# Attention scores of two heads issued together, alternating between the two partition halves

## What is computed

```python
# fox, and alike for the others: scores of the queries [start, end) with the keys [0, end)
s = jnp.einsum('bqhd,bkhd->bhqk', q[:, start:end], k[:, :end]).astype(jnp.float32) * scale
bias = c[:, :, start:end, None] - c[:, :, None, :end]      # fox only: c = cumsum(log_sigmoid(f))
p = jax.nn.softmax(jnp.where(mask, s + bias, -jnp.inf), axis=-1)
outs.append(jnp.einsum('bhqk,bkhd->bqhd', p.astype(v.dtype), v[:, :end]))
# index heads: rel = relu(iq . ik); score = sum over heads of rel * iw; top_k picks the keys of dsa
```

## Time and profile before

| | us |
|---|---|
| median of 3 runs | 2168.05 |
| lowest, highest | 2159.57, 2171.18 |
| the profiled execution | 2163.28 |
| its span | 2161.6 |
| PE busy in the span | 2056.4 (95%) |
| DVE busy | 1469.4 (68%) |
| ACT busy | 976.2 (45%) |

### The profile page before, as it was taken

How to read it: one execution, slowest core, us unless ns; L and a number is a source line. 1 busy time by engine, 2 the same in 40 slices (tenths; PEclk the granted TensorE clock), 3 DMA queues, 4 the chain that set the end, 5 groups by cost and what they waited for, 6 DMA issues and landing times.

```text
span 2161.6 us, 35906 instructions
## 1 busy us (share of the span) xinstructions
PE 2056.4 (95%) x13708; PEld 1878.8 (87%) x13708; DVE 1469.4 (68%) x2592; ACT 976.2 (45%) x1464; POOL 36.9 (2%) x72
## 2 busy tenths in 40 slices
PE   7999999999999999999989997998899979898998
PEld 6999998879998999998879996897789968787997
DVE  7776557677767776557678776765766668566665
ACT  5334444643344344544644344554444445544443
POOL 0000000000000000000000000000000000000000
PEclk9999999999999999999999998996999999878999
DMA  8774443157764774442247762530345544213553
GB/s 303 274 264 165 176 156 109 68 185 277 276 237 160 277 283 183 159 166 101 85 169 274 275 224 97 180 116 32 135 176 194 187 153 152 103 68 125 187 185 135
DMA packets 76906, 382.15 MB, mean 177 GB/s; under 512 B 8960, under 2 KB 9088, under 8 KB 55552
## 3 DMA queue, kind: packets, MB, share of 16 engines
q1 hardware_dynamic: 67392, 329.78, 41.6%
q0 software_dynamic: 9408, 50.90, 6.8%
HBM read 379.60 MB, written 1.05 MB: 176 GB/s over the span
## 4 chain that ended last, share of the span: by engine, by line
PE 87%; DVE 8%; ACT 3%; issue 2%; DMA 0%; SPq 0%; DVEq 0%; ACTq 0%
PE psum L534 26%; PE psum L535 26%; PE psum L536 26%; DVE weights_low_a L1280 2%; PE psum L718 1%; PE psum L713 1%; PE psum L780 1%; PE psum L805 1%; PE psum L807 1%; PE psum L806 1%; PE psum L833 1%; DVE h_low L1331 1%; ACT weights_high_a L955 1%; PE psum L627 1%; PE psum L625 1%
## 5 line engine op out<-in xcount | busy, mean ns | idle before, releaser
L534 PE MATMUL psum<-h_high,weights_high_a 128*128 128x256 f32 x2480 | 713.3, 288 | 15.8 <-DVE h_low L1327 7.7
L535 PE MATMUL psum<-h_low,weights_high_a 128*128 128x256 f32 x2480 | 705.2, 284 | 0.0
L536 PE MATMUL psum<-h_high,weights_low_a 128*128 128x256 f32 x2480 | 704.6, 284 | 0.0
L1280 DVE TENSOR_TENSOR weights_low_a<-raw_a,weights_high_a 128x2048 fp32r<-128x2048 f32 (+1 forms) x232 | 460.1, 1984 | 108.4 <-ACT weights_high_a L955 105.8
L534 PEld LDWEIGHTS psum<-h_high,weights_high_a 128*128 128x128 f32 x2480 | 478.3, 193 | 31.3 <-issue 12.1
L535 PEld LDWEIGHTS psum<-h_low,weights_high_a 128*128 128x128 f32 x2480 | 479.0, 193 | 7.0 <-issue 1.0
L536 PEld LDWEIGHTS psum<-h_high,weights_low_a 128*128 128x128 f32 x2480 | 478.5, 193 | 0.0
L955 ACT ACTIVATE weights_high_a<-raw_a 128x2048 fp32r<-128x2048 f32 (+1 forms) x232 | 387.1, 1669 | 160.5 <-PE psum L536 157.2
L1280 DVE TENSOR_TENSOR weights_low_b<-raw_b,weights_high_b 128x1024 fp32r<-128x1024 f32 x224 | 273.6, 1221 | 78.5 <-ACT weights_high_b L955 77.4
L955 ACT ACTIVATE weights_high_b<-raw_b 128x1024 fp32r<-128x1024 f32 x224 | 237.5, 1060 | 162.2 <-PE psum L536 162.2
L534 PE MATMUL psum<-weights_high_b,gated_high 128*128 128x512 f32 x608 | 241.1, 397 | 0.0
(11 more groups left out here) (276 smaller groups left out, 2897.0 us busy)
## 6 DMA issues: line engine op xcount, KB each, us to landing
ada_weights<-in_w_ada POOLq DMA_DIRECT2D x64, 768.0 KB, 5.1
raw_a<-in_w_ffn_a_a SPq DMA_DIRECT2D x44, 1024.0 KB, 7.2
raw_a<-in_w_ffn_b_a SPq DMA_DIRECT2D x44, 1024.0 KB, 7.3
raw_a<-in_w_ffn_a SPq DMA_DIRECT2D x64, 512.0 KB, 4.5
raw_b<-in_w_ffn_b SPq DMA_DIRECT2D x64, 512.0 KB, 3.5
raw_a<-in_w_proj_a SPq DMA_DIRECT2D x28, 1024.0 KB, 5.7
raw_a<-in_w_gate_a SPq DMA_DIRECT2D x26, 1024.0 KB, 4.7
raw_b<-in_w_ffn_a_b SPq DMA_DIRECT2D x44, 512.0 KB, 3.6
```

The costliest lines, as they stand in the source:

```text
L534: pe.matmul(out, l_hi, r_hi, start=start, stop=False, skip_group_check=True)
L535: pe.matmul(out, l_hi, r_lo, start=False, stop=False, skip_group_check=True)
L536: return pe.matmul(out, l_lo, r_hi, start=False, stop=stop, skip_group_check=True)
L1280: dve.tensor_tensor(wlo[kind][:, p, 0:width], raw[kind][:, p, 0:width], whi[kind][:, p, 0:width].bitcast(F32), ALU.subtract).then_inc(lo_r ...
```

## The change

Heads h and h+1 (h even) of one kind that stand next to each other in the list of items are a pair: their scores are issued together in the first one's tick, product by product in turns, each head into its own bank (ticks t and t+1 have different banks). `scores_ready` (or `prep_ready` for idx) is still raised once per head, by its last product; for fox the forget products of the first half also take turns, those of the second half are issued head by head. The waits of both ticks (`bank_free` for t and t+1) stand ahead of the pair, so it waits for item t-1 to be read besides item t-2. The second head's tick then has no scores on PE. In block 1 kv moves ahead of fox 0, so that fox 0 and fox 1 are neighbours at ticks 2 and 3. Single heads (sb 4, dsa 4) stay as they were. DVE's and ACT's code is the same but for the name of the bank constant and the place of fox 0 and kv in the list.

```diff
-    items = [("ckv", 0), ("fox", 0), ("kv", 0), ("fox", 1), ("turn", 0), ("turn", 1)]
+    items = [("ckv", 0), ("kv", 0), ("fox", 0), ("fox", 1), ("turn", 0), ("turn", 1)]
...
+def paired(items, tick):
+
+    kind, h = items[tick]
+    return kind in HEADS + ("idx",) and h % 2 == 0 and tick + 1 < len(items) and items[tick + 1] == (kind, h + 1)
...
-                while back >= 0 and items[back] is None:
-                    back -= 2
                 if back >= 0:
...
+            def scores(blk, items, ticks_):
+
+                with_forget = items[ticks_[0]][0] == "fox"
+                last = {}
+                for tick in ticks_:
+                    q, k_ = score_operands(items[tick])
+                    pe.matmul(ps[:, SCORE_BANKS[tick % 2], 0:P], q[:, 0:P], k_[:, 0:P], start=True,
+                              stop=not with_forget, skip_group_check=True)
+                if with_forget:
+                    for tick in ticks_:
+                        pe.matmul(ps[:, SCORE_BANKS[tick % 2], 0:P], fcast[:, items[tick][1], 0, :],
+                                  consts[:, C_U:C_U + P], start=False, stop=True, skip_group_check=True)
+                for tick in ticks_:
+                    q, k_ = score_operands(items[tick])
+                    last[tick] = pe.matmul(ps[:, SCORE_BANKS[tick % 2], P:3 * P], q[:, P:SEQ], k_[:, 0:SEQ], start=True,
+                                           stop=not with_forget, skip_group_check=True)
+                for tick in ticks_:
+                    if with_forget:
+                        bank, h = SCORE_BANKS[tick % 2], items[tick][1]
+                        pe.matmul(ps[:, bank, P:3 * P], fcast[:, h, 0, :], consts[:, C_U:C_U + SEQ],
+                                  start=False, stop=False, skip_group_check=True)
+                        last[tick] = pe.matmul(ps[:, bank, 2 * P:3 * P], fcast[:, h, 1, :], consts[:, C_U:C_U + P],
+                                               start=False, stop=True, skip_group_check=True)
+                    if items[tick][0] == "idx":
+                        last[tick].then_inc(now().prep_ready, 1)
+                    else:
+                        last[tick].then_inc(now().scores_ready, 1)
...
             def item_scores(blk, items, tick):
                 kind, h = items[tick]
-                bank = 2 + tick % 2
-                bank_free(items, tick)
+                if tick and paired(items, tick - 1):
+                    return
+                both = (tick, tick + 1) if paired(items, tick) else (tick,)
+                for t in both:
+                    bank_free(items, t)
...
+                if kind in HEADS or kind == "idx":
+                    scores(blk, items, both)
+                    return
+                bank = SCORE_BANKS[tick % 2]
```

More of the change, by code:

```diff
@@ L55 @@
 ROW_BANKS = 6
+SCORE_BANKS = (2, 3)
 P1_G, P1_GKV, P1_BF, P1_GIDX, P1_WKV, P1_END = 0, 24, 25, 31, 95, 223
@@ L709, in bank_free, with score_operands @@
                     pe.wait_ge(s, count_upto(items, back, lambda k: READ_BY[k] == kind))
[L711 to L725, removed]
+            def score_operands(item):
+                kind, h = item
+                q, k_ = {"fox": lambda: (qk1[:, 0, h // 2, :], qk1[:, 1, h // 2, :]),
+                         "sb": lambda: (qk1[:, 2, h // 2, :], qk1[:, 3, h // 2, :]),
+                         "idx": lambda: (tt1[:, h // 2, :], tt1[:, 2, :]),
+                         "dsa": lambda: (tt1[:, 4 + h // 2, :], tt1[:, 3, :]),
+                         "swa": lambda: (tt2[:, h // 2, :], tt2[:, 4 + h // 4, :]),
+                         "moba": lambda: (tt2[:, 6 + h // 2, :], tt2[:, 10 + h // 2, :])}[kind]()
+                pb = HD * (h % 2)
+                return q[pb:pb + HD, :], k_[pb:pb + HD, :]
@@ L734, in item_scores @@
                 if kind in ("kv", "idx", "dsa", "swa", "moba"):
-                    before = max(i for i in range(tick) if items[i] and items[i][0] in ("ckv", "kv", "turn"))
+                    before = max(i for i in range(tick) if items[i] and items[i][0] in PREP and items[i][0] != "idx")
                     pe.wait_ge(now().prep_copied, count_upto(items, before, lambda k: k in PREP))
+                if kind in HEADS or kind == "idx":
+                    scores(blk, items, both)
+                    return
+                bank = SCORE_BANKS[tick % 2]
                 m = None
[L739 to L756, removed]
                 if kind == "ckv":
```

## The result

The changed kernel takes 2142.03 us, median of 4 runs from 2140.90 to 2143.64; the kernel before took 2167.77 beside it. The ratio is 0.9893, 95% interval [0.9872, 0.9914]; the quotient of the two medians, 0.9881, lies inside it. The forecast was 2144, "faster". The profiled execution has a span of 2140.0 us, against 2161.6.

What follows compares the result with a forecast made beforehand. PE was taken as the bound, except in the second half of block 1's ticks. Two layers of 6.5 us (block 2) and 4.4 us (block 1) take 21.8 off 2165.7: 2144, own range 2134 to 2153, with rivals 2129 to 2157.

Steps and rivals of the forecast that it cites:

- Costs of a head and of a pair: Scores on PE: a plain head 1.04 us, fox head 2.31; pairing saves 1.03 per plain pair, 1.42 per fox pair.
- c = 0.22 and s = 0.19: On PE, us for 128 columns of an f32 product, and us lost per switch between 64-row and 128-row products.
- The two equations: PE cost of one head's scores: plain 3c + 2s = 1.04 us, fox 7c + 4s = 2.31 us.
- Block 2 with gate tiles, 4.1 per layer: Four swa pairs at ticks 2, 5, 7 and 9 save 1.03 us each, 4.1 per layer.
- Block 2 without them, 2.4 per layer: Ticks 16 to 25: pairs at 19 and 21 drop 1.58 us each, other engines take back 0.7; 2.4 left.
- Block 1, 4.9 up to tick 14, 4.4 at the end: Per layer, pairs up to tick 14 gain 4.9 us; later savings become PE waits, the tail takes 0.5, leaving 4.4.
- the ring of the earlier trace: Block 1's sb heads: DVE and ACT wait for each other (1.15, 1.88 us) without PE; later PE savings become waits.
- The clock as a rival, 0.08: New PE waits bring more 1.2 GHz time, five us more per layer, costing 10 us: 2154; chance 0.08.
- one of the signs of being wrong: Wrong if half-clock stretches grow, PE waits for score reading at gated pairs, or block 1's last ticks move 10 us.
- Moves: Block 1: kv ahead of fox 0, with fox turn, values and DVE work moved earlier, costs 0; kv's cover 0.5 us.
- Sum: Whole kernel: two layers of 6.5 us (block 2) and 4.4 us (block 1), 21.8 us saved, giving 2144.
- The forecast's base: Time of the kernel before, 2165.7 us: the middle of its profiled execution, 2163.28, and its three-run median, 2168.05.

Runs made afterwards that it cites:

- one half only: Changed kernel, but both heads of a pair and single odd heads read partitions 0 to 63, so the halves can't overlap; 2158.03 us, ratio 0.9955.
- the six layers above: Block 1's two layers in two profiles of the changed kernel (2142.03, 2143.43 us) and one with pairs in block 1 only (2159.08 us).
- The light kernels: The kernel before and the changed kernel, each without block 1's selection rounds and sb stick scans on DVE; 2164.66 us (0.9997) and 2134.10 us (0.9862).

## Why the prediction was right

**Costs of a head and of a pair.** Right. The 1.05 for a plain pair came from the earlier trace rows, measured 1.04; the 3.20 for a fox pair from c = 0.22 and s = 0.19, measured 3.20. With one half only these say 6c + 2s = 1.70 for a plain pair; measured, 1405.06 - 1403.12 - 0.24 = 1.70. For a fox pair they say 14c + 4s = 3.84, and 3.84 is measured there too. The two equations as printed, 1.04 and 2.31, give c = 0.23 and s = 0.18; with those the three would be 3.2, 1.7 and 3.9, so the rounding decides nothing. That s is the price of a switch between 64 and 128 rows is the model's reading; what the runs show is that it fits three more cases.

**Block 2 with gate tiles, 4.1 per layer.** Measured 3.8, by the copies and by PE itself. From PE's starts, the ticks that lost their scores give back 1.04, 1.04, 0.81 and 0.99 (ticks 3, 6, 8 and 10), and each pair costs 0.01 more than a head. The 0.81 is a first small wait for ACT: at tick 8 the values start 0.19 behind the last product of the turn, at 1420.18, where it is 0.11 at tick 10, and ACT's turned copy had ended at 1420.13.

**Block 2 without them, 2.4 per layer.** Three layers of the two profiles of the changed kernel have 86.0, that is 6.2 - 3.8 = 2.4, as forecast. PE's timeline, ticks 15 to 19, first layer (answers to the earlier trace rows):

```profile
1448.90 0.60 PE L742 MATMUL psum<-turned_two 64*128 64x256 f32 x4
1452.16 0.49 PE L734 MATMUL psum<-turned_two 64*128 64x128 f32 x4 [2.66 <-DVE negated_row_max L1523]
...
1458.09 0.69 PE L823 MATMUL psum<-tokens_two,probs_turned_two 128*128 128x64 f32 x2 [3.55 <-ACT probs_turned_two L1161]
```

The pair at tick 17 waits 2.66, where its first head waited 0.72: the "2 us later" of the forecast. It costs nothing: the values behind it start 66.44 us after the layer's first gate copy, where before it was 70.28 (1467.43 - 1397.15), the same 3.8 us earlier as ahead of the pair. The list of signs said "no wait of PE for L1505 at the pairs" in block 2, which contradicts this and was worded too widely; at the gated pairs it is so.

In the remaining layer the ticks took 84.17, so the part without gate tiles gained 4.2 instead of 2.4. There the granted clock came back to full while the ticks were running, and in the second profile, same code, it didn't. The windows (us, busy of PE, PEld, DVE, ACT, POOL, clock, DMA), first profile, then the second:

```profile
1464.00:1470.50 6.50, 4.65 (x35) 3.53 (x35) 3.37 (x19) 5.60 (x20) 0.00 (x0) 0.97 0.01 1
```

```profile
1458.00:1482.00 24.00, 20.00 (x89) 16.67 (x90) 8.79 (x47) 15.74 (x42) 0.00 (x0) 0.50 0.13 45
```

The forecast's "clock as before, at half from the first stall on" holds in the main for three layers of four: there it stays at half to the end of the ticks, from the pair's wait on in one and from the wait for ACT's copy behind it in two. All three took 86.0, with 26.1 or 20.0 us at half clock, so the 6 us between those two waits cost nothing. The change isn't the cause of the difference between the two profiles, as both have it. That the clock is, is read off four layers, no run set it; the 2 us of the 84.17 are luck, and the forecast didn't need them.

**Block 1, 4.9 up to tick 14, 4.4 at the end.** Measured -4.8 at tick 14; the lead at ticks 7, 9, 11 and 14 was forecast as 1.4, 2.5, 3.5, 4.9 and measured as 1.4, 2.4, 3.5, 4.8. Of what is saved behind that, nothing was to be kept, and nothing was: the lead rose to 5.8 at tick 16 and was 4.6 from tick 17 to 23, and 4.1 and 4.6 us were left at the end. The 4.4 allowed 0.5 for the tail; the layers lost 0.5 and 0.0 there, the more the longer the tail ran at half clock (the six layers above). DVE's stretch from fox 4 to sb 0 is the same work in the same time, before 11.15 busy of 11.70:

```profile
345.70:357.40 11.70, 11.70 (x101) 11.21 (x100) 11.17 (x32) 6.13 (x14) 0.00 (x0) 1.00 0.38 136
```

Then the ring of the earlier trace rows, unchanged: DVE waits 1.15 for ACT at 358.54, ACT waits 1.88 for DVE at 371.50. The chain of waits goes through it as the forecast said, in pieces of DVE and ACT with no PE between (start us, us, what):

```profile
370.90 0.57 DVE scores L1559
371.47 0.02 issue
371.50 0.03 ACT scores L1122
371.52 0.40 issue
371.92 0.37 ACT gates_one L1167
372.29 1.80 ACT weights_high_a L973
```

and PE waits for what comes behind it:

```profile
369.67 0.43 PE L823 MATMUL psum<-tokens_one,probs_turned 128*128 128x64 f32 x2 [1.72 <-ACT probs_turned L1161]
```

The light kernels show DVE's part by experiment: with less on DVE the pairs gave 8.4 to 9.2 us instead of 4.1 to 4.6.

**The clock as a rival, 0.08.** The half-clock stretches in block 1's ticks did grow, from 6.4 and 7.4 us to 13.7 and 8.8, which was one of the signs of being wrong; in block 2's they shrank, from 25.2 and 26.1 to 15.9 and 20.0. In the second profile it is 14.2, 8.4, 26.1 and 20.0. Behind the wait at 369.67, the 24 products of a gate tile run from 370.36 to 374.69, 4.33 us where 24 x 0.12 = 2.9 is usual:

```profile
371.00:374.40 3.40, 3.40 (x18) 3.40 (x17) 1.85 (x5) 2.90 (x4) 0.00 (x0) 0.51 0.28 111
```

A clock of 0.51 is the lower of the two levels, 1.2 GHz. PE had stood still twice before, 0.45 and 1.72 us. Such a drop stands in three of the six layers with the changed ticks and in no layer of a kernel without pairs; the same two waits stand in all six, so they are not enough to bring it. It cost nothing here, since ACT reaches this tile's copy only at 377.75, behind its own wait for DVE: the ring had room, and the gate copies of ticks 17 to 23 come 4.6 us earlier in the layer without the drop too. What the earlier fall of the clock in the tail cost is at most the 0.8 us between the six layers above. The mean granted clock is 0.959 in both kernels.

**Moves.** kv and the second bank priced at 0: right, by experiment and by the margins.

**Sum.** 21.8 forecast; the columns give 22.9 and 20.9, the profiled spans 21.6, the medians 25.7; the interval of the ratio is 18.6 to 27.7 us (0.86 to 1.28% of 2167.77). The forecast's base, 2165.7, was 2 us below the median of the kernel before in the same session, and its time 2 us above the changed kernel's. By the medians the gain was 3.9 us larger than forecast; that the forecast time is off by only 2 is partly luck, as the base was too low by as much again. By the columns, which a few us outside the ticks don't reach, the 21.8 lies between the two profiles.

## What to carry to other kernels

Two f32 matmuls with 64 rows each, on the two partition halves and into two banks, cost as much as one if no 128-row product stands between them (two heads in one bank were not tried); plain ones need only be neighbours in the queue, those with 128-row products in them must take turns. What it is worth is read off not by PE's busy time but by the place: here 32.5 us less PE work gave 21 to 26 us, because from the first stretch in which DVE has no gap the lead is only passed on. Before such a stretch nearly every saved us counted; behind it, the other engines' ring sets the pace, and reordering DVE moved its idle time to ACT.

## What the hardware showed that I hadn't expected

- A layer's ticks in block 2 took 84.17 or 86.02 us for the same instructions: 84.17 where the granted clock came back to 0.97 in the ticks without gate tiles, 86.02 where it stayed at 0.50.
- Behind waits of 0.45 and 1.72 us the granted clock fell to 0.51 over a gate tile in the middle of dense work in three layers, and behind the same waits it didn't in three others.
- In a plain pair the like passes of the two heads start 0.01 us apart, in whichever order the heads' products were issued.
- Outside the ticks, profiled spans of one and the same kernel differed by 6 us (2140.0, 2146.0), with its ticks equal but for 2 of them; a sum of a few us is better tested on the stretch that is changed than on the whole.
